# Encoder layer on one core: window keys and queries turned in the projection, output weights loaded during window attention, reciprocals spread by TensorE, the first feed-forward blocks written to SBUF

## The reference

```python
h = rmsnorm(x, g_pre_mix);  proj = h @ w_in                    # 1024 -> 1536, cut into q_A k_A v_A q_B k_B v_B
# A: 8 heads, 2 key heads, q and k normed per head and rotated; every query sees all 2048 keys
s = einsum(q, k) * 64**-0.5;  p = softmax(s);  o_A = p @ v
# B: 8 heads, 2 key heads; 128-query blocks over 384 keys, |i-j| <= 128
s = einsum(q, k) * 64**-0.5 + bias_table[t5_bucket(rel)]       # -1e30 outside the band
m = max(max(s), sink);  p = exp(s - m);  o_B = p @ v / (sum(p) + exp(sink - m))
mix = concat(o_A, o_B) @ w_o;  x = x + rmsnorm(mix, g_post_mix)
u = relu(rmsnorm(x, g_pre_ffn) @ w_ffn_up);  f = (u * u) @ w_ffn_down   # 1024 -> 4096 -> 1024
out = x + rmsnorm(f, g_post_ffn)
```

## Time and profile before

| | us |
|---|---|
| median of 3 runs | 2890.35 (2888.19 to 2890.84) |
| profiled execution | 2890.22 |
| its span, first to last instruction | 2888.6 |
| PE busy | 2705.4 (94%) |
| DVE busy | 1827.9 |
| ACT busy | 1429.2 |
| POOL busy | 803.3 |

### The profile page before, as it was taken

One profiled execution on the slowest core, in us unless ns is written; L12 is line 12 of the kernel. 1 busy time (PEld: TensorE's weight loads), 2 busy tenths in 40 slices (PEclk: granted clock), 3 DMA queues, 4 the chain that ended last, 5 costly groups with the idle time before them and its releaser, 6 DMA issues. The chain is left out here.

```text
span 2888.6 us, 36041 instructions
## 1 busy us (share of the span) xinstructions
PE 2705.4 (94%) x12274; PEld 2185.6 (76%) x12274; DVE 1827.9 (63%) x2503; ACT 1429.2 (49%) x2122; POOL 803.3 (28%) x603
## 2 busy tenths in 40 slices
PE   7999599999999978988995999999998999999998
PEld 5888467777777747976874888788886888888887
DVE  5666499999999947865556666675653343343433
ACT  3222177777777747973334544554443333233332
POOL 1111178888888854541110000000000000000000
PEclk9999799999999989998997999999999999999999
DMA  5333421111111122327876333533325445355442
GB/s 181 107 108 102 122 67 30 31 34 28 35 30 32 23 75 70 84 67 218 207 202 216 124 117 97 209 107 100 114 92 189 171 172 182 121 196 179 172 172 98
DMA packets 295611, 338.16 MB, mean 117 GB/s; under 512 B 73059, under 2 KB 219635, under 8 KB 293292
## 3 DMA queue, kind: packets, MB, share of 16 engines
q1 hardware_dynamic: 269980, 317.92, 35.7%
q10 hardware_dynamic: 23552, 13.64, 1.5%
q0 software_dynamic: 1936, 4.74, 0.6%
HBM read 234.10 MB, written 97.86 MB: 115 GB/s over the span
## 5 line engine op out<-in xcount | busy, mean ns | idle before, releaser
L126 PE MATMUL d_pr<-d_w_hi,d_s_hi 128*128 128x512 f32 x1024 | 399.7, 390 | 11.6 <-DVE d_s_lo L1872 11.6
L1871 DVE TENSOR_TENSOR d_w_lo<-d_w_raw,d_w_hi 128x1024 fp32r<-128x1024 f32 x128 | 156.8, 1225 | 386.2 <-ACT d_s_hi L1848 382.3
L127 PE MATMUL d_pr<-d_w_lo,d_s_hi 128*128 128x512 f32 x1024 | 399.5, 390 | 0.0
L128 PE MATMUL d_pr<-d_w_hi,d_s_lo 128*128 128x512 f32 x1024 | 399.3, 390 | 0.0
L644 POOL TENSOR_TENSOR p_sum<-p_sum,p_hi 128x1024 f32<-128x1024 f32 x160 | 383.3, 2396 | 37.0 <-issue 19.7
L126 PE MATMUL u_pr<-u_t_hi,u_w_hi 128*128 128x512 f32 x896 | 351.2, 392 | 32.3 <-DVE u_t_lo L1687 31.9
L127 PE MATMUL u_pr<-u_t_lo,u_w_hi 128*128 128x512 f32 x896 | 350.1, 391 | 0.0
L128 PE MATMUL u_pr<-u_t_hi,u_w_lo 128*128 128x512 f32 x896 | 350.1, 391 | 0.0
L676 ACT ACTIVATE p_hi<-s_ps 128x1024 fp32r<-128x1024 f32 x256 | 263.3, 1028 | 157.0 <-PE s_ps L767 155.7
L720 DVE TENSOR_TENSOR p_lo<-s_ps,p_hi 128x1024 fp32r<-128x1024 f32 x256 | 312.5, 1221 | 29.5 <-ACT s_ps L677 22.3
L704 DVE TENSOR_REDUCE part_max<-m_ps 128x1 f32<-128x1024 f32 x251 | 304.6, 1214 | 33.1 <-PE m_ps L749 32.9
(11 more groups left out here) (219 smaller groups left out, 5384.5 us busy)
## 6 DMA issues: line engine op xcount, KB each, us to landing
d_w_raw<-in_w_ffn_down SPq DMA_DIRECT2D x128, 512.0 KB, 3.8
u_w_raw<-in_w_ffn_up SPq DMA_DIRECT2D x32, 1024.0 KB, 6.0
act_blocks<-u_s_out SPq DMA_DIRECT2D x128, 256.0 KB, 6.2
d_s_lo<-act_blocks SPq DMA_DIRECT2D x128, 256.0 KB, 2.7
u_t_lo<-h_blocks SPq DMA_DIRECT2D x14, 1024.0 KB, 10.9
x_in<-in_x SPq DMA_DIRECT2D x16, 512.0 KB, 4.3
q_split<-q_out ACTq DMA_DIRECT2D x16, 512.0 KB, 3.3
q_turned<-w_raw SPq DMA_DIRECT2D x16, 512.0 KB, 3.4
```

Of the source, the lines that this page charges most:

```text
L126: nc.tensor.matmul(out, stat_hi, mov_hi, start=first, stop=False)
L127: nc.tensor.matmul(out, stat_hi, mov_lo, start=False, stop=False)
L128: return nc.tensor.matmul(out, stat_lo, mov_hi, start=False, stop=last)
L1871: nc.vector.tensor_tensor(w_lo[:, n % SLOTS], w_raw[:, n % RAW], w_hi[:, n % SLOTS].bitcast(F32), ALU.subtract)
```

## The change

**Project.** B's queries and keys are turned too (`turn_qk(t, s, 1)`, 10 more transposes per tile) and stored turned; `q_split` and `k_split` are gone.

**Global.** B's bias is built here: table product ahead of the first maxima, bias row and its reversed copy moved by SP, the 8 `flip` products between the maxima and the first scores, the result stored at n == 0. POOL's sum is split by ACT (`sum_high`, u == 3) and DVE (`sum_low`, end of u == 4), and `total` is two fp32r matmuls at u == 6 instead of a float32 one at u == 4.

**Window.** Keys and queries come turned; query transposes, their two ACT copies and the DVE copy `mark` (L1077) are gone; queries have 4 buffers; all 32 steps are written out. SP also loads w_o (8 DMAs) and the first two tiles' inputs of the next stage, all ahead of the load of queries 3.

**Mix.** w_o is already in SBUF. The reciprocals come as a hi and a lo row for even and odd heads; a matmul with 0/1 weights (`pick`) spreads them, and DVE multiplies (`scale_heads`). POOL's product is gone. x, `t_out` have one buffer; x1, xn and h live in `wo_raw`. Blocks of the first group go by DMA into `ffn_up`'s SBUF tile `u_t_lo`; `ffn_up`'s first weights are loaded at tile 8.

```diff
@@ project
-                sp.wait_ge(qk_kept, t + 1)
-                sp.dma_start(q_cols[t], qk_t[:, s, 0:8]).then_inc(qk_stored[s], 16)
-                sp.dma_start(k_cols[t], qk_t[:, s, 8:10]).then_inc(qk_stored[s], 16)
+                for b, turned in enumerate((qk_t, qkb_t)):
+                    sp.wait_ge(qk_kept, 2 * t + b + 1)
+                    sp.dma_start(q_cols[t][:, 8 * b:8 * b + 8], turned[:, s, 0:8]).then_inc(qk_stored[s], 16)
+                    sp.dma_start(k_cols[t][:, NG * b:NG * b + NG], turned[:, s, 8:10]).then_inc(qk_stored[s], 16)
...
-                act.dma_start(scratch["q"].rearrange("(h t) p c -> t p h c", t=NT)[t], q_out[:, s]).then_inc(stored[s], 16)
-                act.dma_start(scratch["k"][t], k_out[:, s]).then_inc(stored[s], 16)
...
             sweep(pe, NT // 2, tile)
-            turn_qk(NT - 1, 1)
+            turn_qk(NT - 2, 0, 1)
+            for b in range(2):
+                turn_qk(NT - 1, 1, b)
@@ attend_global
+            def sum_high(n):
+                act.wait_ge(added, ADDS * (n + 1))
+                at_least(act, sum_used, n)
+                nc.scalar.activation(sum_hi[:], p_sum[:, n % 2, 0:QB], ACT.Copy).then_inc(sum_hi_made, 1)
...
+                    if u == 3 and n > 0:
+                        sum_high(n - 1)
...
+            def sum_low(n):
+                dve.wait_ge(sum_hi_made, n + 1)
+                nc.vector.tensor_tensor(sum_lo[:], p_sum[:, n % 2, 0:QB], sum_hi[:].bitcast(F32), ALU.subtract).then_inc(sum_lo_made, 1)
...
+                    if u == 4 and n > 0:
+                        sum_low(n - 1)
...
-                pe.wait_ge(added, ADDS * (n + 1))
-                nc.tensor.matmul(ob_ps[:], ones_high[:], p_sum[:, n % 2, 0:QB], start=alone, stop=alone).then_inc(sum_used, 1)
+                pe.wait_ge(sum_lo_made, n + 1)
+                nc.tensor.matmul(ob_ps[:], ones_high[:], sum_hi[:], start=alone, stop=False)
+                nc.tensor.matmul(ob_ps[:], ones_high[:], sum_lo[:], start=False, stop=alone).then_inc(sum_used, 1)
...
+            pe.wait_ge(row_moved, 32)
+            pe.wait_ge(row_ready, 1)
+            for h in range(8):
+                at_least(pe, bias_ready, h - 1)
+                nc.tensor.matmul((oa_ps, ob_ps)[h % 2][:, 0:SPAN], flip[:], bias_rev[:, h], start=True, stop=True).then_inc(bias_product, 1)
+            pe.wait_ge(bias_ready, 8)
...
-                    if u == 4 and n > 0:
+                    if u == 6 and n > 0:
                         total(n - 1, False)
@@ attend_window
+            for k in range(KT):
+                sp.dma_start(scratch["w_o_raw"][:, k], w_o_tiles[k]).then_inc(ahead_loaded, 16)
+            sp.wait_ge(rd_filled, 1)
+            sp.wait_ge(rden_stored, 32)
+            for t in range(2):
+                sum_and_scale_loads(sp, scratch, t, t, ahead_loaded)
...
-                    nc.vector.tensor_copy(mark[:, h:h + 1], sink[:, head:head + 1])
...
-                    if h == 0 and not known(n, TOTAL - 2):
-                        turn_q(n + 2, s, b + 1)
@@ mix_heads
-                nc.gpsimd.tensor_tensor(hn[:, s], sums[:, s], scales[:, s], ALU.mult).then_inc(hn_made, 1)
+            def scale_heads(t, s):
+                dve.wait_ge(scaled, t + 1)
+                nc.vector.tensor_tensor(sums[:, s], sums[:, s], scale[:], ALU.mult).then_inc(hn_made, 1)
+            def spread_scale(t, s, p):
+                at_least(pe, sums_loaded[s], 64 * p)
+                at_least(pe, hn_made, t)
+                nc.tensor.matmul(scale[:].rearrange("p j c -> p (j c)"), pick[0:HD + 33], rd[0:HD + 33, s].rearrange("p j c -> p (j c)"),
+                                 start=True, stop=True).then_inc(scaled, 1)
...
+                    to = t_first[:, i, o] if i < NT // 4 else t_tiles[i - NT // 4, o]
+                    sp.dma_start(to, blocks[o]).then_inc(h_stored[s], 16)
```

More of the change, by code:

```diff
@@ L300, in tile @@
                     xt_high(t + 1, 1 - s)
+                if not (isinstance(t, int) and t < 2):
+                    keep_turned(t - 2, s, p - 1, 1)
                 evacuate(t, s, p, 1)
@@ L466, in tile @@
                     turn(t + 1, 1 - s)
+                if not (isinstance(t, int) and t < 2):
+                    turn_qk(t - 2, s, 1)
                 chunk(t, s, 1)
                 chunk(t, s, 2)
-                turn_qk(t - 1, 1 - s)
+                turn_qk(t - 1, 1 - s, 0)
             sweep(pe, NT // 2, tile)
-            turn_qk(NT - 1, 1)
+            turn_qk(NT - 2, 0, 1)
+            for b in range(2):
+                turn_qk(NT - 1, 1, b)
 def attend_global(nc, a, scratch):
@@ L693, in _ @@
             keep_b(TOTAL - 1)
+            sum_high(TOTAL - 1)
             act.wait_ge(sum_used, TOTAL)
@@ L817, in _, with sum_and_scale_loads @@
             total(TOTAL - 1, True)
+def sum_and_scale_loads(eng, scratch, t, s, landed):
+    sums = scratch["o_t"].rearrange("(j e) p (t c) -> t e p j c", e=2, c=P)
+    for e in range(2):
+        eng.dma_start(scratch["sums"][e * HD:(e + 1) * HD, s], sums[t, e]).then_inc(landed, 16)
+    for part in range(2):
+        rows = scratch["rden"][part].rearrange("(j e) (t c) -> t e j c", e=2, c=P)
+        eng.dma_start(scratch["rd"][part * HD:(part + 1) * HD:32, s].bitcast(F32), rows[t]).then_inc(landed, 16)
 def attend_window(nc, a, scratch):
@@ new lines, in load_q, with load_bias @@
+            def load_q(n):
+                at_least(sp, scores_done, GRP * (n - QS + 1))
+                b, g = n // NG, n % NG
+                heads = slice(8 + GRP * g, 8 + GRP * (g + 1))
+                dest = (q_all[:, n % QS], q_one[0:HD, n % QS])
+                for tile, rows in zip(dest, (slice(0, 2 * HD), slice(HD, 2 * HD))):
+                    sp.dma_start(tile.bitcast(F32).rearrange("p (h c) -> p h c", h=GRP), q_cols[b][rows, heads]).then_inc(q_loaded[n % QS], 16)
+            def load_bias(g):
+                heads = slice(GRP * g, GRP * (g + 1))
+                sp.dma_start(bias[:, heads], scratch["bias"][:, heads]).then_inc(bias_in[g], 16)
@@ L919, in step @@
             def step(n, g, b):
-                if not known(n, TOTAL - 2):
-                    load_q(b + 1, g)
+                if n + 3 < TOTAL:
+                    load_q(n + 3)
                 if not (isinstance(n, int) and n < 4):
                     store(n - 4, b - 2, g)
-            sweep(sp, NT, step, 2)
+            every(sp, NT, step)
             for n in range(TOTAL - 4, TOTAL):
                 store(n, n // NG, n % NG)
+                if n == TOTAL - 3:
+                    for g in range(NG):
+                        sp.wait_ge(stored[g], 16 * (NT - 2))
+                    for t in range(2):
+                        sp.dma_start(scratch["heads"][:, t], scratch["mix"][t]).then_inc(ahead_loaded, 16)
@@ L983, in _ @@
                 load_v(0, g)
-            pool.wait_ge(const_in, 80)
+            nc.gpsimd.memset(scratch["rd"][:].bitcast(F32), 0.0)
+            nc.gpsimd.memset(scratch["pick"][:].bitcast(F32), 0.0)
+            pool.drain()
+            for part in range(2):
+                for e in range(2):
+                    row = 2 * HD * part // 2 + 32 * e
+                    last = nc.gpsimd.memset(scratch["pick"][row:row + 1, e * HD:(e + 1) * HD].bitcast(F32), 1.0)
+                    if part == 1 and e == 1:
+                        last.then_inc(rd_filled, 1)
+                    pool.drain()
+            pool.wait_ge(const_in, 32)
             gap(0, 0)
@@ L994, in step @@
                     load_v(b + 1, s)
-            sweep(pool, NT, step, 2)
+            every(pool, NT, step)
             denominator(TOTAL - 1, 1)
@@ L1046, in step @@
                     exponentials(n + 1, 1 - s)
-            sweep(act, NT, step, 2)
+            every(act, NT, step)
             keep_o(TOTAL - 2, 0)
@@ L1109, in step @@
                 low(n, s)
-            sweep(dve, NT, step, 2)
+            every(dve, NT, step)
             finish(TOTAL - 2, 0, NT - 1)
@@ L1212, in step @@
                     weigh(n - 1, 1 - s)
-            sweep(pe, NT, step, 2)
+            every(pe, NT, step)
             turn_o(TOTAL - 2, 0)
@@ L1509, in tile @@
             def tile(t, s, p):
+                if not known(t, NT - 1):
+                    spread_scale(t + 1, 1 - s, p + s)
                 if isinstance(t, int) and t == 0:
```

475 lines of the change are left out of this document (216 added, 259 removed).

## The result

The changed kernel takes 2998.68 us (median; 2990.25 to 3000.87) where the kernel before takes 2890.6: a ratio of 1.037 (95% interval 1.0351 to 1.0389), slower by 108 us. The forecast was 2920, with a range of 2880 to 2966. The profiled execution spans 2998.4 us, 109.8 more than before.

| stage | before | after | difference | forecast |
|---|---|---|---|---|
| project | 338.8 | 359.8 | +21.0 | +21.4 |
| attend_global | 713.1 | 801.0 | +87.9 | +39.6 |
| attend_window | 240.8 | 235.0 | -5.8 | -18.5 |
| mix_heads | 241.9 | 254.5 | +12.6 | -4.5 |
| ffn_up | 639.6 | 633.8 | -5.8 | -8 |

What follows compares the result with a forecast made beforehand. Each stage was taken to be set by PE's work plus its waits, with DVE's order counting in attend_global's blocks. The terms 15.4 + 6 + 6.5 + 32 + 1.1 - 18.5 - 10.5 + 6 - 8 gave +30: 2920, range 2880 to 2966.

Steps and rivals of the forecast that it cites:

- Blocks of attend_global: Deciding term: sum_low lengthens the chain and total is exposed at u == 6, +1.07 for each of 30 blocks, +32.
- case A: The main forecast: attend_global blocks go from 21.2 to 22.3 us, total 2920, own range 2905 to 2938; chance 0.40.
- rival C: attend_global: B's hold plus half clock after PE's idle time, 1.7 more per block, 3008; chance 0.08.
- B: Rival in attend_global: POOL first, combine holds sum_low in every block, +69 in place of +32, 2957; chance 0.20.
- D: Rival in attend_global: sum_low slips into a pause, moving total wins 0.40 per block, 2876; chance 0.20.
- E: Rival in attend_global: sum_low costs nothing but total's 0.46 per block is exposed, +14, 2902; chance 0.12.
- Project: Ten more transposes per tile on PE, +15.4, and more transpose cycles at the stage's end, +6.
- Start of attend_global: Eight flip products now on PE's only path before the first scores, +6.5; ends 4 and 8.
- attend_window: Earlier first pt_hi -23, mark gone -2.3, stall of 7 from added loads; -18.5, ends -25 and -8.
- Start of mix_heads: With w_o already in SBUF the first product comes earlier and a second wait shrinks: -10.5, ends -8 and -12.
- The steady part: mix_heads: spread_scale adds 3.5 to PE, waits for scales move from POOL to PE, 2.5; +6.
- Handover to ffn_up: First group's blocks and first weights need no DRAM load, so ffn_up starts earlier: -8, ends -6 and -9.

Runs made afterwards that it cites:

- e5: Changed kernel with the products for the row maxima at u == 5 made twice, as useless PE work: 2980.6 us, ratio 1.0312.
- e9: Changed kernel with the products for the row maxima at u == 5 made four times, as useless PE work: 2951.26 us, ratio 1.0202.
- e10: Kernel before with only its float32 total moved from u == 4 to u == 6: 2930.76 us, ratio 1.0135.
- e1: Changed kernel with the two products of total moved from u == 6 to u == 5: 2941.98 us, ratio 1.0186.
- e3: Changed kernel with the negation of the maxima on ACT instead of DVE: 2965.69 us, ratio 1.0271.
- e4: Kernel before with only the negation of the maxima on ACT instead of DVE: 2857.56 us, ratio 0.9891.
- e6: Changed kernel with attend_window's denominators loaded right behind keys 0 and next-stage loads issued one per step: 2980.72 us, ratio 1.0313.
- e7: Changed kernel with PE's spread_scale of the next tile in mix_heads behind the first chunk of products: 2968.59 us, ratio 1.0274.

## Why the prediction was wrong, by its steps

**Blocks of attend_global (+32 forecast, +76.5 measured): the step that failed.** (The stage is 801.0, less 36.6 ahead of the first scores and 13.0 behind the last ones; before 713.1, 26.2, 12.0.) Its two parts held together: blocks at full clock take 22.3 us, which is the 21.2 + 1.07 of the forecast (one block of the changed kernel, six in e5, nearly all in e9), and `sum_low` lengthens the chain by 0.61. The step that failed is the idle time, "with an idle PE of about 1.1 ahead of the scores", and with it the price of the clock, which case A put at nothing. The 1.1 counted 0.50 + 0.62 and forgot that `total`, when it leaves u == 4, leaves its own 0.87 behind as idle time: 0.49 + 0.62 + 0.87 = 1.98, measured 1.94. e10 shows the 0.87 alone. The 1.07 was right as a delay and wrong as a description of PE's time. The clock was priced for rival C alone, at up to 3.3 us of idle time; the one row looked at had 3.57. It fell in nearly every block at 1.94. 27 blocks x 1.57 = 42 us, of the 44.5 beyond the forecast. That the idle time is the cause is shown by e9, which only adds work inside it: the idle time falls to 0.6, the low stretches go in all 30 blocks, and the blocks take the 22.3 of full clock. e1, e5 and e10 agree: each had fewer low stretches with less idle time. The Trainium skill, page "TensorE: Matmul & The Clock Gate", section "HAM oscillation — how this bites in real kernels", describes a loop whose wait recurs in every round and brings the clock down in every one; the 27 blocks agree with the recurrence. The waits of its loop are longer, about 3 to 5 us, and for a DMA; the 1.94 us here, set by DVE's order, and the 1.35 of e10 brought the clock down too. So the page alone wouldn't have given case A this price, and the measured rows decide.

**Rival C** came nearest in time (3008), by a right mechanism and a wrong condition: B, on which it built, didn't hold. That its time comes close to 2998.68 is luck: it adds a hold of 1.24 per block that wasn't there to a low clock in all 30 blocks. Where the subtraction of DVE and the `combine` of POOL start together (573.20, 573.21), POOL waited, as in the row of mix_heads. The one behind was held by the one that came first, and not for long: 0.5 us, where the subtraction took 0.68. That order decides is also what the Trainium skill says, page "SBUF — State Buffer", section "Who interferes with whom": issue order, not the shape of an operation, decides who is blocked; these rows and e3's agree. The forecast's "waits for the whole of the other" is a little too much for its own row as well, 2.33 - 1.29 = 1.04 beside a sum of 1.22. The hold by POOL's sum, which the forecast read out of the 1.58 of `neg_max`, is shown by e3 (it passes to the subtraction behind it) and e4 (without either, 33 us less). It was used to explain 1.4 us per block in the kernel before and not seen as the larger gain that lay there.

**Rivals D and E** are out: with `sum_low` on DVE the chain to the scores was 0.61 longer, and no such block was shorter than 21.2 us. Two slips in the rivals' working change nothing: B's block would be 21.2 + 2.31 = 23.5 us, not 23.6, and D counts 31 blocks where the other terms count 30.

**Project (+21.4, measured +21.0)**: right, with the cycle at the end too; four `keep` stood 3.79 apart, the last at 354.22.

**Start of attend_global (+6.5, measured +10.4, first scores 36.6 us in against 26.2)**: under-sized, beyond its upper end of 8. The eight `flip` products began at 387.5 and the scores at 396.3, 8.8 us later, where the forecast had 6.14 + 0.4: the first products were 1.3 to 1.4 apart at a granted clock of 0.54, the later ones 0.8 at 1.00, while the row of before was at 1.00 throughout (6.14). What else is in the 10.4 wasn't looked into, and none of it was tested apart. The end (+1.1) was right: 13.0 against 12.0.

**attend_window (-18.5, measured -5.8)**: the steps' gain was right (5.83 against 5.91). The first `pt_hi` came at 34.5 and not 25.5, and the stall was 10.9 and not 7. The forecast let the loads run at one rate from the stage's start, 22 us at most. SP issued those of the denominators only 16.3 us in, behind the keys, and DVE could go on 12 us later. e6 showed it: with these loads early the first `pt_hi` came 11.4 us earlier.

**Start of mix_heads (-10.5)** was right: the first product came 8.5 us earlier, and the thirteenth, behind the second wait for the split weights, 10.5 (12.50 us in against 23.05). The forecast's own two numbers, -8.2 and -1.9, add up to -10.1. **The steady part (+6, measured +23.1)** was not right. The step "it makes PE wait where POOL did" held, and its ends were 0 and +31; the value chosen, 2.5, had no better reason than that the loads are issued ahead. They are, but behind seven stores every other tile, and PE waited 3.2 us for them in each of five tiles: 16.0. Four of these waits brought the clock down too; e7 has neither.

**Handover to ffn_up (-8)**: -6.5 at the first product, 5.8 us into the stage in place of 12.3, and -5.8 over the stage, just under the forecast's lower end of 6.

Sum of the misses: 44 in the blocks, 4 at their start, 13 in the window, 17 in mix, 2 in ffn_up: 80, as between 110 and 30.

Left open: which blocks get a low stretch and which don't. Their share isn't ordered by the idle time ahead of the scores alone (22 of 30 at 1.50, 13 at 1.65), and in the changed kernel, once it had begun, it came in every block. Whether the longest idle piece counts or all idle time nearby wasn't separated either.

## What to carry to other kernels

Work that is hidden in a wait isn't only free, it also fills the wait. Before moving it elsewhere, write down what idle time it leaves behind, and add that to the idle time that the rest of the change makes. When a change lengthens PE's idle time in a repeated block, as here from 0.5 to 1.9 us, price the low clock for each block (here 1.57 us) beside the delay itself, and look at the granted clock first when a block is slower than its instructions explain. A tiny DVE instruction with a long duration beside a running POOL instruction is a gain to be had, if another engine waits for what stands behind it: give it to an engine that isn't in the way, and look at what moves up into its place, since that can be held in its stead (here the subtraction, while the reduction wasn't). And when a stage's difference is read as the worth of an edit, look at the untouched stages too.

## What the runs showed of the hardware

- More work made the kernel faster: with the pair of products at u == 5 made four times, it took 47 us less, 41 of them in the stage of the edit (e9).
- A block that spends 3.4 us at 1.2 GHz takes 1.57 us longer (23.87 against 22.30 in e5), a little less than half of 3.4. In the changed kernel the low stretches start 23.89 us apart, nearly the length of the blocks that they make (23.85).
- Idle times of PE in blocks with such a stretch were as short as 1.35 in 8 of 30 blocks (e10), and 0.59 brought none (e9); e1, with pieces of 0.82 and 0.40, had 4.
- The negation of 128x4 into fp32r takes DVE 0.17 us when POOL is quiet (the shortest of the earlier trace rows, the first), 1.6 beside POOL's sum, and ACT 0.20 beside the same sum (e3, e4). A reduction of 128x8 to 128x4 on DVE takes 0.16 beside that sum.
